# The turns of the probabilities behind the value products in the steady rounds of four attentions

## What is computed

```python
def reference(x, c, norm_g, ...):
    x = first_block(...)      # layer 0: nsa_mixer, layer 1: dilated_mixer
    return second_block(...)  # layer 2: MLA + SWA, SwiGLU; layer 3: forgetting + chunk, SwiGLU
```

```python
s = (q @ k.T) * scale + bias      # 256 x 256, at most the part up to the query's tile
p = exp(s - max(s))
o = (p @ v) / sum(p)
```

```python
p_cmp = masked_softmax(s_cmp, cmask)
o_cmp = einsum('btghn,bngd->btghd', p_cmp, v_cmp)
o = gates[..., 0:1] * o_cmp + gates[..., 1:2] * o_slc + gates[..., 2:3] * o_win
```

## Time and profile before

| | us |
|---|---|
| median of 3 runs | 987.42 (986.91 to 987.93) |
| the profiled execution, its own time | 988.05 |
| its span, first to last instruction | 986.2 |
| nsa, rounds 2 to 14 | 115.1 to 175.4 in the span |
| dil, rounds 0 to 9 | 304.9 to 334.5 |
| ab and cd | 415 to 440 and 736 to 763 |

### The profile page before, as it was taken

One profiled execution on the slowest core, in us unless ns is written; L12 is line 12 of the kernel. 1 busy time (PEld: TensorE's weight loads), 2 busy tenths in 40 slices (PEclk: granted clock), 3 DMA queues, 4 the chain that ended last, 5 costly groups with the idle time before them and its releaser, 6 DMA issues.

```text
span 986.2 us, 15101 instructions
## 1 busy us (share of the span) xinstructions
PE 954.4 (97%) x5656; PEld 805.9 (82%) x5656; DVE 647.3 (66%) x1166; ACT 471.4 (48%) x733; POOL 179.4 (18%) x152
## 2 busy tenths in 40 slices
PE   5999899989999999999999999999999999999996
PEld 2799666868886889988888888879999888888885
DVE  4656567975764775667767666676446776766665
ACT  1353577535445645573344444444547334444442
POOL 2015237213960401130000000010024000000001
PEclk9999999999999999999999999999999999999998
DMA  9965555434565246223366565534532336555541
GB/s 374 363 232 169 215 212 184 158 129 173 207 220 189 87 179 237 86 86 130 136 256 208 209 205 189 188 143 163 199 126 89 129 135 249 185 190 187 189 184 43
DMA packets 24105, 178.37 MB, mean 181 GB/s; under 512 B 3792, under 2 KB 4224, under 8 KB 7928
## 3 DMA queue, kind: packets, MB, share of 16 engines
q1 hardware_dynamic: 19840, 166.70, 45.6%
q0 software_dynamic: 2224, 8.94, 2.7%
q10 hardware_dynamic: 1991, 2.07, 0.8%
HBM read 176.65 MB, written 1.05 MB: 180 GB/s over the span
## 4 chain that ended last, share of the span: by engine, by line
PE 84%; DVE 8%; DMA 3%; ACT 3%; issue 1%; POOL 0%; SPq 0%; DVEq 0%; ACTq 0%; POOLq 0%
PE G L1102 12%; PE G L1103 12%; PE G L1104 12%; PE S L1222 8%; PE T L1222 8%; PE S L1221 4%; PE T L1221 3%; PE T L621 2%; PE T L526 2%; PE G L1302 2%; PE G L1291 2%; PE G L1283 2%; PE G L631 1%; PE G L630 1%; PE G L629 1%; DMA early<-in_ada_w 1%
## 5 line engine op out<-in xcount | busy, mean ns | idle before, releaser
L2297 DVE TENSOR_TENSOR wlo<-ring,whi 128x2048 fp32r<-128x2048 f32 x88 | 154.4, 1759 | 88.4 <-ACT whi L1861 54.7
L1102 PE MATMUL G<-whi,hTh 128*128 128x308 f32 (+3 forms) x480 | 163.9, 341 | 0.3 <-DVE hTl L567 0.3
L1103 PE MATMUL G<-wlo,hTh 128*128 128x308 f32 (+3 forms) x480 | 161.0, 335 | 0.0
L1104 PE MATMUL G<-whi,hTl 128*128 128x308 f32 (+3 forms) x480 | 161.0, 335 | 0.0
L2159 DVE TENSOR_TENSOR wlo<-ring,whi 128x1024 fp32r<-128x1024 f32 (+3 forms) x66 | 105.4, 1634 | 66.4 <-ACT whi L1719 66.2
L1222 PE MATMUL S<-hT,whi 128*128 128x512 f32 x336 | 122.1, 397 | 0.0
L1222 PE MATMUL T<-hT,whi 128*128 128x512 f32 x336 | 120.6, 394 | 0.0
L1102 PEld LDWEIGHTS G<-whi,hTh 128*128 128x128 f32 x480 | 90.2, 188 | 10.9 <-DVE hTl L567 2.4
L1719 ACT CAST whi<-ring 128x1024 fp32r<-128x1024 f32 (+3 forms) x66 | 75.1, 1186 | 44.9 <-PE G L1104 30.1
L1856 ACT CAST whi<-ring 128x2048 fp32r<-128x2048 f32 x44 | 83.9, 1906 | 25.1 <-PE S L1325 17.4
L1103 PEld LDWEIGHTS G<-wlo,hTh 128*128 128x128 f32 x480 | 90.4, 188 | 5.6 <-issue 0.7
(11 more groups left out here) (386 smaller groups left out, 1880.9 us busy)
## 6 DMA issues: line engine op xcount, KB each, us to landing
ring<-in_ffn SPq DMA_DIRECT2D x44, 1536.0 KB, 6.5
ring<-in_dil_w_in SPq DMA_DIRECT2D x16, 1024.0 KB, 4.8
ring<-in_cd_w_in SPq DMA_DIRECT2D x10, 1232.0 KB, 5.5
ring<-in_ada_w SPq DMA_DIRECT2D x12, 1024.0 KB, 6.8
early<-in_ada_w SPq DMA_DIRECT2D x8, 1024.0 KB, 10.0
ring<-in_nsa_w_in SPq DMA_DIRECT2D x5, 1432.0 KB, 6.1
ring<-in_ab_w_in SPq DMA_DIRECT2D x4, 1440.0 KB, 6.2
vec<-in_vecs POOLq DMA_DIRECT2D x11, 512.0 KB, 5.3
```

The lines of the kernel that those rows point to most:

```text
L1102: pe.matmul(out_, act_h, w_h, start=first_, stop=False)
L1103: pe.matmul(out_, act_h, w_l, start=False, stop=False)
L1104: return pe.matmul(out_, act_l, w_h, start=False, stop=last_)
L2297: TT(wlo[b][:, part], ring[:, b, part], whi[b][:, part].bitcast(F32), ALU.subtract).then_inc(st[what + "_lo"], 1)
```

## The change

In rounds 2 <= p < pairs - 1, called steady, T(p) moves from its place behind S(p) to a place behind PV(p). It still stands ahead of `after(p)`. This holds for 13 rounds of nsa and 5 rounds each of dil, ab and cd, 28 in all. Nothing is added or removed, and the programs of DVE, ACT, POOL and SP are the same.

```diff
-                if 1 <= p < pairs + 1:
+                steady = 2 <= p < pairs - 1
+                if 1 <= p < pairs + 1 and not steady:
                     for j in (2 * p - 2, 2 * p - 1):
                         turn_probs(j)
...
                     for j in (2 * p - 4, 2 * p - 3):
                         times_v(j)
+                if steady:
+                    for j in (2 * p - 2, 2 * p - 1):
+                        turn_probs(j)
                 if after is not None:
                     after(p)
```

## The result

The changed kernel took 989.50 us, the median of 18 runs, beside 987.93 us for the kernel before in 18 runs that took turns with it. The ratio is 1.0023 with a 95% interval of 1.0015 to 1.0030, so the change costs 1.5 to 3.0 us. The ratio is not the quotient of the two medians, which are 1.57 us apart (1.0016); the same holds for the ratios further down. It leaves out one run of the kernel before that took 1191.3 us, and has in it two of the kernel after at 994.6 and 994.7 us, whose granted clock was 0.992 and 0.993. The 14 runs of the kernel after with a mean granted clock of 0.997 or more have a median of 989.4, so the cost is not one of the clock. The forecast was 989.3 us and +1.9. The profiled execution of the changed kernel took 989.19 us with a span of 987.4, where that of before had 988.05 and 986.2.

What follows compares the result with a forecast made beforehand. PE, busy in 97% of the span, was taken as the bound. Terms +2.0 + 0.6 + 0 - 0.6 - 0.1 = +1.9 us on a median of 987.42 gave 989.3 us, range 986.0 to 991.0.

Steps and rivals of the forecast that it cites:

- The pairs of rounds 8 to 13: Three pairs of nsa rounds, each going from 9.21 to 9.87 us, +0.66 each and +2.0 us in all.
- POOL holds L2566: In nsa, DVE's 128x4 product comes up 0.14 us after POOL's add began and waits until 4.59 us.
- rival A: In nsa's pairs POOL doesn't hold DVE's small product: -1.0 for +2.0, sum -1.1 us, time 986.3; chance 0.22.
- The alternative value: An nsa pair whose small product isn't held by POOL takes 8.88 us, 0.33 under before.
- Rounds 6 and 7: In nsa, one turn moves behind L(7) while the DVE chain keeps its length: +0.66 less 0.1, so +0.6 us.
- Rounds 2 to 5: In nsa, 0.66 us lost at L(2) is given back at round 4: together about 0, at most -0.1.
- Round 14: Round 14 and the end of nsa: no block waits, turns and value products swap at equal cost, 0.
- dil: Round 2 comes 0.4 us early and later rounds save 0.1 per two rounds: -0.6 us, between -0.4 and -0.7.
- rival B: Each move of the turns costs a switch on PE over 28 rounds: +3.5 us in sum, 991; chance 0.14.
- ab and cd: Steady rounds stay equal; second turns no longer wait for the second copy: -0.1 us for both.
- Rival D: Whole kernel: new waits and old ones cancel, nothing shows, 987.4 us; chance 0.07.
- C (faster): Earlier takes end nsa, dil and the output projections sooner; with unheld products the sum is -2.5, 984.9 us; chance 0.07.

Runs made afterwards that it cites:

- e4: Changed kernel with POOL's near adds cut to one column, 511 of 512 columns left out; 987.75 us, ratio 0.9999.
- e6: Changed kernel with DVE's small product reading PSUM and one SBUF tile, the reciprocal taken second, nothing left out; 986.55 us, ratio 0.9988.
- e3: Changed kernel with POOL's adds of a round waiting until DVE has taken that round's pair; 989.31 us, ratio 1.0016.
- e9: Kernel before with the turns moved only in rounds 2 to 7 of nsa; 988.60 us, ratio 1.0009.
- e11: Same as e6, but rounds 2 and 6 of nsa keep the old order of turns; 986.00 us, ratio 0.9985.
- e1: Kernel before with the turns moved only in dil, ab and cd, nsa in the old order; 987.48 us, ratio 0.9996.
- e2: Kernel before with the turns moved only in the steady rounds of nsa; 990.79 us, ratio 1.0025.
- e10: The kernel of e6 a second time in other runs; 986.83 us, ratio 0.9991.

## Why the prediction was right

The sign and the mechanism of the largest term were those of the forecast. That the time was only 0.2 us off is in part luck. The forecast started from 987.42, where the kernel before measured 987.93 beside the changed one, and of the six terms four were too low or too hopeful: by their traces they add to +2.4 and not +1.9. Step by step:

- **The pairs of rounds 8 to 13**, the largest term, were to cost 0.66 us each. They cost 0.61 each (9.82 against 9.21). L(11) stood at 5.82 as worked out, with PE idle for 1.04 us rather than 1.16. The size is off because C and PV(10) start 0.96 us apart now, 0.1 more than the piece I had taken from the earlier trace rows, and L(11) to S(12) is 4.00 rather than 4.05.
- **POOL holds L2566** in the new order: shown by the kernel after, and by e4, e6 and e3, which take the hold away in three different ways. The page that the prediction drew on (the Trainium skill, SBUF — State Buffer, "SBUF: two separate sides") agrees: the same product with one operand in PSUM took 0.164 us at most in all 96 instances of the six kernels that have it so. The margin between the two starts was 0.24 us and not 0.14, again the 0.1 of C and PV, so rival A was less near than its chance of 0.22 said.
- **The alternative value** of an unheld pair, 8.88, was measured at 8.92 and 8.93.
- **Rounds 6 and 7**: +0.6 predicted; +0.59 from S(6) to S(8) in the kernel after and in e9. The size and the place of T(7) were right, but one reason was wrong: "POOL holds L2566 here too". In the kernel after (POOL, DVE and PE in time) the small product of round 6 comes up as POOL's first add ends and takes 0.17 us:

```profile
135.13 0.49 PE L640 MATMUL S<-kT,qT 64*128 64x128 f32 x4
...
138.87 2.63 POOL L989 TENSOR_TENSOR bias<-bias,near 128x512 f32<-128x512 f32 x2 [1.19 <-ACT near L2004]
...
140.20 0.17 DVE L2570 TENSOR_TENSOR rden<-rden,gate 128x4 f32<-128x4 f32 x1
...
141.60 1.06 PE L439 MATMUL G<-ring,cb 128*32 128x512 f32 x8
```

  L(7) is 6.47 us behind S(6), 6.49 before, and with the product that can't be held (e6) S(6) to S(8) is still 10.46. What sets these two rounds is the DVE chain behind C(6) without any hold.
- **Rounds 2 to 5**: predicted as given back in full. S(3) was 0.61 us later relative to S(2), and S(6) 0.2. These 0.2 were L(4)'s wait for a transfer of weights that wasn't there before; in e9, without it, the difference is 0.00. e11 shows that both halves of this term were real: with the loss at L(2) avoided, the gain behind it is 0.6.
- **Round 14**: 0 predicted, +0.05 measured (S(14) to S(15) 3.00 against 2.95).
- **dil**: the 0.4 of round 2 came as worked out. Here are DVE's copy, L(2) and S(3) of the kernel after, beside the earlier trace rows:

```profile
311.30 1.28 DVE L558 COPY kT<-G 128x512 f32<-128x512 f32 x2
...
312.63 1.92 PE L439 MATMUL G<-ring,cb 128*32 128x512 f32 x16 [0.26 <-DVE kT L558]
...
317.49 0.49 PE L640 MATMUL G<-kT,qT 64*128 64x128 f32 x4
```

  S(0) to S(3) is 10.95 us against 11.39, and 10.95 again in e1. The further 0.2 that I gave to the later rounds was wrong: S(3) to S(7) went from 11.90 to 11.99. It was an estimate from the spread of T behind S, with no wait in a row behind it. Rounds where nothing waited went from 2.94 or 2.95 to 3.00, so a move of T does cost some 0.05 us; what in the order costs it was not tested. That is about half of what rival B gave a round, but nsa's pairs, where the waits decide, show none of it.
- **ab and cd**: -0.1 predicted; from S(0) to S(7) ab went from 20.61 to 20.64 us and cd from 20.61 to 20.72. This is small but comes from the change: cd has 20.71 in e1, where its turns are moved, and 20.61 in e2, where they aren't. The second turns that were to save 0.1 had no wait to save.

The terms measured in the traces add to +2.68 - 0.35 + 0.1 = +2.4 us, against +1.9 predicted and 1.5 to 3.0 in the timed runs. Rival D (nothing shows) and C (faster) are outside the interval of 1.0015 to 1.0030. What the prediction left out altogether is the clock: it named the longer wait of L(2) but put no price on a wait beyond its length. In the profile of after the clock didn't fall behind it, so the sum came out right there; in e2, with the same nsa, it did, and S(2) to S(8) took 1.47 us more than after's, 1.38 of it from S(6) to S(8).

## What to carry to other kernels

When a step leaves the shade of a wait, ask which wait ends there next, and whether its chain got shorter by the same edit. Here PE did its part earlier, and a product on 128x4 elements behind another engine's add gave all of it back; removing that hold (an operand from PSUM instead of a second one from SBUF) turned a loss of 0.61 us into a gain of 0.29 over the kernel before. Judge order round by round, since the same move gained 0.6 us over rounds 3 to 5, cost 0.6 in round 2 and again in round 7, and in round 6 showed only through the clock. Prefer filler work ahead of a long wait of PE, because a wait of 1.5 us can cost about as much again through the clock (1.1 to 1.4 us in five of seven executions here).

## What I had not expected of the hardware

- The granted clock fell to its lower level for some 3 us in or behind PE waits of 1.5 to 1.8 us in five of seven executions, but not in the other two with the same waits. In e6 it fell during the wait, 0.6 us before PE went on, and in e10 1.6 us after PE had gone on. What decides between the two outcomes stays open.
- The transfer of dil's first weights took 4.73 to 6.83 us on the critical chain, whatever the kernel. This spread of 2.1 us is about as large as the whole effect of the change.
- POOL's adds kept their length (1.27 us each) in every kernel that has them whole, also when DVE's small product was waiting for the first of them; in the rows read it was DVE that gave way when POOL had started first.
